# The first attention of a two-block kernel, put in steps between the products of the eight query and key units

## The reference, cut to what matters

```python
def first_block(x, ...):
    h = rms_norm(x, attn_pre_norm)
    x = x + rms_norm(hybrid_mixer(h, ...), attn_post_norm)
    h = rms_norm(x, ffn_pre_norm)
    return x + rms_norm((silu(h @ w_gate) * (h @ w_up)) @ w_down, ffn_post_norm)

def hybrid_mixer(h, ...):
    dq, dk, dv, nq, kc, vc, ks, vs, kw, vw, gt = split(h @ w_in)
    # differential attention: 4 heads, two maps each, values of width 128
    a = softmax(q0 @ k0) - lam * softmax(q1 @ k1)      # causal, queries in blocks of 128
    o_diff = rms_norm(a @ v, diff_subln) * (1 - lam_init)        # head by head
    # sparse attention: 8 query heads in 2 groups, three gated branches
    kcmp, vcmp = compress(kc), compress(vc)            # silu(blocks @ w1) @ w2
    o_nsa = g0 * attn(q, kcmp, vcmp) + g1 * attn(q, ks, vs) + g2 * attn(q, kw, vw)
    return concat([o_diff, o_nsa]) @ w_out
```

## Time and profile before

| | us |
|---|---|
| median of 3 runs (1918.52 to 1919.34) | 1919.23 |
| the profiled execution | 1918.23 |
| its span | 1916.3 |
| PE busy in it | 1875.6 (98%) |
| POOL busy in it | 1241.5 (65%) |
| DVE busy in it | 820.6 (43%) |
| ACT busy in it | 436.3 (23%) |
| mean granted TensorE clock | 0.993 |

### The profile page before, as it was taken

One profiled execution on the slowest core, in us unless ns is written; L12 is line 12 of the kernel. 1 busy time (PEld: TensorE's weight loads), 2 busy tenths in 40 slices (PEclk: granted clock), 3 DMA queues, 4 the chain that ended last, 5 costly groups with the idle time before them and its releaser, 6 DMA issues.

```text
span 1916.3 us, 25712 instructions
## 1 busy us (share of the span) xinstructions
PE 1875.6 (98%) x9416; PEld 1511.1 (79%) x9416; DVE 820.6 (43%) x1396; ACT 436.3 (23%) x893; POOL 1241.5 (65%) x747
## 2 busy tenths in 40 slices
PE   8999999999999999999999999999999999999997
PEld 6886568888888898767888888889787888888886
DVE  6346864533331045253543334004994463334103
ACT  4344862211110021132311111003334331111000
POOL 7975546866676558653876667666656686666662
PEclk9999999999999999999999999999999999999999
DMA  6341002323232214211242323221323223333311
GB/s 207 122 131 45 2 1 78 98 89 99 88 120 96 91 45 154 88 46 44 78 119 89 99 88 126 96 75 56 109 67 99 77 88 97 89 99 108 106 61 44
DMA packets 44878, 168.28 MB, mean 88 GB/s; under 512 B 4984, under 2 KB 7288, under 8 KB 44672
## 3 DMA queue, kind: packets, MB, share of 16 engines
q1 hardware_dynamic: 44496, 164.56, 27.7%
q10 hardware_dynamic: 304, 2.64, 0.4%
HBM read 165.07 MB, written 2.11 MB: 87 GB/s over the span
## 4 chain that ended last, share of the span: by engine, by line
PE 87%; DVE 5%; POOL 5%; issue 2%; ACT 1%; DMA 0%; POOLq 0%; SPq 0%; DVEq 0%
PE psum L527 27%; PE psum L528 26%; PE psum L529 26%; POOL w_lo L421 2%; DVE h_lo L1413 1%; DVE tmp L1455 1%; PE psum L723 1%; DVE e_ring L1570 1%; PE psum L709 1%; POOL w_hi L418 1%; PE psum L574 1%; POOL e_ring L467 1%; PE psum L783 1%; PE psum L804 1%; PE psum L750 1%
## 5 line engine op out<-in xcount | busy, mean ns | idle before, releaser
L421 POOL TENSOR_TENSOR w_lo<-raw,w_hi 128x1024 fp32r<-128x1024 f32 (+1 forms) x286 | 749.6, 2621 | 23.8
L527 PE MATMUL psum<-h_hi,w_hi 128*128 128x512 f32 (+1 forms) x1780 | 677.4, 381 | 13.6 <-POOL w_lo L421 7.1
L529 PE MATMUL psum<-h_hi,w_lo 128*128 128x512 f32 (+1 forms) x1780 | 670.7, 377 | 0.0
L528 PE MATMUL psum<-h_lo,w_hi 128*128 128x512 f32 (+1 forms) x1780 | 670.6, 377 | 0.0
L418 POOL TENSOR_SCALAR w_hi<-raw 128x1024 fp32r<-128x1024 f32 (+1 forms) x286 | 323.0, 1129 | 484.1 <-PE psum L529 460.2
L527 PEld LDWEIGHTS psum<-h_hi,w_hi 128*128 128x128 f32 x1780 | 334.7, 188 | 88.4 <-issue 13.8
L529 PEld LDWEIGHTS psum<-h_hi,w_lo 128*128 128x128 f32 x1780 | 334.1, 188 | 68.9
L528 PEld LDWEIGHTS psum<-h_lo,w_hi 128*128 128x128 f32 x1780 | 334.3, 188 | 66.9 <-issue 0.2
L527 PE MATMUL psum<-g_hi,w_hi 128*128 128x512 f32 (+1 forms) x594 | 219.5, 369 | 0.0
L528 PE MATMUL psum<-g_lo,w_hi 128*128 128x512 f32 (+1 forms) x594 | 218.9, 369 | 0.0
L529 PE MATMUL psum<-g_hi,w_lo 128*128 128x512 f32 (+1 forms) x594 | 218.9, 369 | 0.0
(11 more groups left out here) (269 smaller groups left out, 1858.1 us busy)
## 6 DMA issues: line engine op xcount, KB each, us to landing
raw<-in_wide SPq DMA_DIRECT2D x239, 512.0 KB, 3.6
raw<-in_down SPq DMA_DIRECT2D x48, 704.0 KB, 4.1
decay<-decay_rows ACTq DMA_DIRECT2D x1, 2048.0 KB, 7.9
out<-x SPq DMA_DIRECT2D x16, 128.0 KB, 1.7
x<-in_xt SPq DMA_DIRECT2D x3, 512.0 KB, 7.0
x<-in_xt ACTq DMA_DIRECT2D x1, 512.0 KB, 4.6
o_diff<-in_angles SPq DMA_DIRECT2D x1, 512.0 KB, 10.3
cols<-in_cols SPq DMA_DIRECT2D x1, 221.0 KB, 4.4
```

The lines of the kernel that those rows point to most:

```text
L421: nc.gpsimd.tensor_tensor(w_lo[:, slot, 0:w], raw[:, j % RAW, 0:w], w_hi[:, slot, 0:w].bitcast(F32), ALU.subtract).then_inc(units_split, 1)
L527: pe.matmul(out_ap, lhs[0], rhs[0], start=first, stop=False)
L528: pe.matmul(out_ap, lhs[0], rhs[1], start=False, stop=False)
L529: return pe.matmul(out_ap, lhs[1], rhs[0], start=False, stop=last)
```

## The change

The 32 units come in another order: value units (dv) before the eight query and key units, compression pairs one feature unit apart. The eight units dq0, dk0, dq1, ... dk3 are last, and 42 of the 48 steps are put between their products, at the places `A_WEAVE`; six steps and the rest of the pipeline follow, the last three stages at columns of the opening. Sparse and differential heads alternate. Scores use banks 2 and 3 only, transpositions of differential steps bank 4 only, since banks 0 and 1 serve the units. The four blocks of compressed scores are computed in one go, their softmaxes run one after another, and their transpositions are two calls in dq0. Sparse outputs are written over queries that are no longer needed (`nsa_out`), the angles have a tile of their own. The norm of the differential heads is done head by head: ACT scales three heads with twelve copies, the fourth comes last. `stay_warm` is gone from this stage.

```diff
-A_STREAM = ["kc", "vc", "vg0", "vg1", "vg2", "nq0", "nq1", "nq2", "ck0", "cv0", "nq3", "ks", "ck1", "cv1", "kw", "dq0", "ck2", "cv2",
-            "dq1", "dq2", "ck3", "cv3", "dq3", "dk0", "w2", "dk1", "dk2", "dk3", "dv0", "dv1", "dv2", "dv3"]
+A_WOVEN = [f"{w}{c}" for c in range(4) for w in ("dq", "dk")]
+A_STREAM = ["kc", "vc", "vg0", "vg1", "vg2", "nq0", "nq1", "ck0", "cv0", "nq2", "ck1", "cv1", "nq3", "ck2", "cv2", "ks", "ck3", "cv3",
+            "kw", "dv0", "w2", "dv1", "dv2", "dv3"] + A_WOVEN
...
-STEPS = DIFF_STEPS + NSA_STEPS
+STEPS = nsa_steps(0) + nsa_steps(1) + diff_steps(0) + nsa_steps(2) + diff_steps(1) + nsa_steps(3, (1,)) + diff_steps(2) + nsa_steps(3, (2,)) + diff_steps(3)
+A_WEAVE = [(3, 5, 6, 7)] + [(1, 3, 4, 6, 7)] * 3 + [(1, 2, 3, 5, 6, 7)] * 3 + [(1, 3, 4, 6, 7)]
+A_WOVEN_STEPS = [[sum(map(len, A_WEAVE[:j])) + k for k in range(len(A_WEAVE[j]))] for j in range(len(A_WOVEN))]
+A_LEFT = A_WOVEN_STEPS[-1][-1] + 1
...
@@ POOL: where the weighing stands among the splits
-                    cuts.insert(0, (A_UNITS + SLOTS, weigh_pairs))
+                    first = A_UNITS - len(A_WOVEN) + SLOTS
+                    rest = [A_WOVEN_STEPS[j][-1:] + (A_WOVEN_STEPS[j + 1][:-1] if j + 1 < len(A_WOVEN) else list(range(A_LEFT, len(STEPS))))
+                            for j in range(len(A_WOVEN))]
+                    cuts[0:0] = [(first, lambda: weigh_pairs(A_WOVEN_STEPS[0][:-1]))] \
+                        + [(first + j + 1, lambda steps=steps: weigh_pairs(steps)) for j, steps in enumerate(rest)]
@@ PE: a step
-                        if t >= 2:
-                            pe.wait_ge(pair_maxed, 2 * (t - 1))
-                        elif t == 1:
-                            pe.wait_ge(v_out, len(TOKEN_MAJOR))
-                        stay_warm(warm.get(t, 0), 2 * (t % 2))
+                    if t:
+                        pe.wait_ge(pair_maxed, 2 * t)
+                    else:
+                        pe.wait_ge(v_out, len(TOKEN_MAJOR))
+                    if kind == "diff" and i == NB - 1:
+                        pe.wait_ge(rope_added, ROPES.index(f"dk{head}") + 1)
...
-                        if r >= 2:
-                            copied(r if kind == "nsa" else r - 1)
+                    if r:
+                        copied(r)
@@ PE: the woven units
+            def woven_pairs():
+                low_start = n.base["h_low"]
+                for j, name in enumerate(A_WOVEN):
+                    if name == "dk0":
+                        pe.wait_ge(cmp_turned, 2)
+                    bank, w = free_bank(name), next_unit()
+                    for t in range(KC):
+                        mm = three(psum[:, bank, :], [w[0](t), w[1](t)], h_of(t), t == 0, t == KC - 1)
+                        if t == KC - 1:
+                            mm.then_inc(unit_done, 1)
+                        if t in A_WEAVE[j]:
+                            pair_step(A_WOVEN_STEPS[j][A_WEAVE[j].index(t)], low_start)
+                        if j == 0 and t in (2, 5):
+                            cmp_turn(t // 5)
+                for t in range(A_LEFT, len(STEPS) + 1):
+                    pair_step(t, low_start)
+                pe.wait_ge(rope_added, len(ROPES))
+                pe.wait_ge(pair_maxed, 2 * len(STEPS))
+                def between(t):
+                    if t < 3:
+                        pair_step(len(STEPS) + 1 + t, low_start)
+                    if t == 2:
+                        turn_diff(0)
+                        turn_diff(1)
+                        turn_diff(2)
+                    if t == 5:
+                        turn_diff(3)
+                w_out((4, 5, 6, 7, 0, 1, 2, 3), nsa_of, between)
@@ PE: the order ahead of them
-            feature("nq2")
             compress(0)
+            feature("nq2")
+            compress(1)
             feature("nq3")
+            compress(2)
             feature("ks")
-            compress(1)
+            compress(3)
             feature("kw")
-            feature("dq0")
...
             for u in token_units("dv", (2, 2, 2, 2), 4 * P):
-                if u in (1, 2):
-                    cmp_turn(u)
-                    cmp_scores(u + 1)
-            cmp_turn(3)
+                if u == 0:
+                    second_layer()
+                if u == 1:
+                    cmp_scores()
+            woven_pairs()
@@ ACT: after dv3
+            for j, name in enumerate(A_WOVEN):
+                for k, t in enumerate(A_WOVEN_STEPS[j]):
+                    if j == 0 and k == 0:
+                        cmp_copy(0)
+                    if j == 0 and k == 1:
+                        cmp_copy(1)
+                    if t == A_WOVEN_STEPS[j][-1]:
+                        shift(name)
+                    pair_step(t)
+            for t in range(A_LEFT, len(STEPS) + PAIR_MIX + 2):
+                pair_step(t)
+                if t == len(STEPS):
+                    diff_root(0, slice(0, 12))
+                if t == len(STEPS) + 1:
+                    scale_diff()
+            turned_high(0)
+            diff_root(1, slice(12, 16))
+            for c in range(1, 4):
+                turned_high(c)
@@ DVE: after the four cmp_softmax
+            for j, name in enumerate(A_WOVEN):
+                for t in A_WOVEN_STEPS[j][:-1]:
+                    pair_step(t)
+                rope_parts(name)
+                pair_step(A_WOVEN_STEPS[j][-1])
+                rope_sum(name)
+            for t in range(A_LEFT, len(STEPS) + PAIR_MIX + 1):
+                pair_step(t)
...
```

More of the change, by code:

```diff
@@ L144, in combined_by_dve, with done_before @@
     return STEPS[t][0] == "diff" and STEPS[t][3] == NB - 1
+def done_before(kind, head):
+    place = next(j for j, end in enumerate(SET_ENDS) if end[1:] == (kind, head))
+    earlier = [end for end in SET_ENDS[:place] if MIX_BANK[end[1:]] == MIX_BANK[kind, head]]
+    return earlier[-1][1:] if earlier else None
 def copies_by_dve(upto):
@@ L605, in last_unit, with opening @@
                 mm.then_inc(unit_done, 1)
-            def opening(order, h):
+            def opening(order, h, before=None):
                 banks, units = [], []
@@ new lines, in diff_root, with scale_diff @@
+            def diff_root(k, sums):
+                act.wait_ge(diff_mean, k + 1)
+                nc.scalar.activation(diff_ms[:, 2, sums], diff_ms[:, 3, sums], ACT.Sqrt).then_inc(diff_rooted, 1)
+            def scale_diff():
+                act.wait_ge(diff_inverted, 1)
+                for head in range(3):
+                    for b in range(NB):
+                        part = dqk[:, head, b * P:(b + 1) * P]
+                        ins = copy(part, part, scale=diff_ms[:, 1, 4 * head + b:4 * head + b + 1])
+                    ins.then_inc(diff_normed, 1)
@@ L1637, in fox_step @@
                     n.take("h_low")
-            def turn_outputs(first, banks, scale=None):
-                for c in range(4):
-                    low_of_bank(first + c, 4 + c % banks, scale)
             v.memset(ones[:], 1.0).then_inc(set_up, 1)
```

480 lines of the change are left out of this document (239 added, 241 removed).

## The result

The changed kernel takes 1925.29 us (median of 7 runs, 1924.12 to 1925.99), the kernel before 1918.96 (7 runs on the same chip, 1917.95 to 1920.49): 1.0032 times as long, with an interval of 1.0020 to 1.0043. That is 6.3 us slower, at a forecast of 11.6 us slower. The profiled execution took 1925.33 us, span 1923.5.

The account below looks back on a forecast made before the run. TensorE, with 87% of the chain, was taken as the bound, with 14 us to win in the first attention. -14 - 0.6 + 9.7 + 5.9 + 4.2 + 6.4 = +11.6 us, about 1930; range 1920 to 1937.

Parts of the forecast that it names:

- Idle time of the stage: First attention stage: TensorE's ramp, warming calls and most waits for softmax work go, minus 14 us.
- The short products: Value and key units before the weaving: four small insertions shrink to one, minus 0.6 us.
- Part 1: Woven units and opening: 46 insertions between products cost about 0.21 us each, 9.7 us; between 0 and 14.
- the trace has the same weaving in the second attention: Step giving the price per insertion: gaps of 0.09 and 0.11 us there, about 0.2 us, taken for every insertion.
- The sign that I named: What would show the insertion price: each woven step shows 0.32 and 0.34 us around it, where the pace is 0.233.
- Rival (b): Stepping in is free: sum +1.9 us, 1921, no change; 0.09 together with a faster case, 0.02 of it faster.
- Part 2: Units before the weaving: waits for low tokens and GpSimd splits plus a half clock delay kw, 5.9 us; 4.8 to 7.
- Part 3: Woven stretch: waits at the start 0.9, at unit ends 1.5, for differential weighing 1.8; sum 4.2 us.
- Part 4: Tail, steps 42 to 49 without products: TensorE waits for maxima, copies and weighings, 6.4 us; between 3 and 10.
- (a): All waits of TensorE covered: minus 4.9 us, 1914, faster; chance 0.08.
- (c): Tail and unit boundaries cost a third of the forecast: +4.6 us, 1924, on the border of no change; chance 0.18.
- (d): Woven stretch: DVE's sparse-step coefficient is locked out by GpSimd's split, +8 us if half shows, 1938; chance 0.15.

Follow-up runs that it names:

- e3: Kernel after plus 24 unread transpositions in the attention's output projection, one behind each triple of three feature units: 1927.66 us.
- e4: Kernel after plus the same 24 unread transpositions in one row behind the three feature units: 1927.59 us.
- e8: Kernel after plus unread small operations of three kinds between triples of the output projection's feature units, then eight of each kind in a row; one profile, not timed.
- e10: Kernel after with the mix ahead of the transposition in each attention step: 1925.85 us, ratio 1.0039 to the kernel before.
- e1: Kernel after with nq2 ahead of the first compress pair, kw ahead of the fourth, hidden-layer turn inside the first value unit: 1924.28 us, ratio 1.0035 to the kernel before.
- e5: Kernel after with ScalarE copying the transposed block before the rotation's shift in each of eight woven units: 1925.92 us, ratio 1.0040 to the kernel before.
- e7: On top of the order of e1, ScalarE makes the high part of the eight compress units instead of POOL: 1920.48 us, ratio 1.0009 to the kernel before.
- e6: Kernel after with VectorE combining the last differential head's two softmaxes, one instruction a step for all four blocks: 1922.89 us, ratio 1.0025 to the kernel before.
- e9: Kernel after with the 64 short products in four stretches of 16, each behind one value-unit tile: 1925.11 us, ratio 1.0034 to the kernel before.
- e2: Kernel after with the 64 short products split, 32 behind the second and 32 behind the third value unit: 1923.72 us, ratio 1.0035 to the kernel before.
- e12: e11 with mix first only in the 42 woven steps, ScalarE's copy ahead of the shift, and two filling products: 1915.68 us, ratio 0.9984 to the kernel before.
- e11: Kernel after with the edits of e1, e7, e9, e6 and e10 together: 1921.51 us, ratio 1.0016 to the kernel before.

## Why the prediction came out as it did

**Direction right, size high by 5 us.** The parts, forecast against measured:

- Idle time of the stage: -14 forecast. In the kernel before it is 10.2 us of stands and 3.4 of warming, so -13.6; the prediction's "14" was rounded up.
- The short products: -0.6 forecast, -1.5 measured. Four stretches of 16 with three turns of the compressed branch between them, and the second layer of the compression, cost TensorE 8.7 us among the products before; the row of 64, one turn and the second layer cost 7.2 after, with 0.9 for the lower clock inside the row in it.
- Part 1, stepping in: +9.7 forecast, about +6 measured. The mechanism was half right. 28 steps end in a sparse mix and pay 0.17 to 0.19 each, some 5; three at the start, with a score alone, pay some 0.2. Steps with a differential mix, cmp_turn and the three stops in the opening pay nothing. The failed step is "the trace has the same weaving in the second attention": there every step ends in a mix on half of the columns, and I carried its price to steps that do not. e3, e4 and e8 showed it, e10 confirmed it by moving the mix. The sign that I named, 0.32 and 0.34 around a step, is there around differential steps too (0.33 and 0.32 around the one at 242.55), which cost nothing: the gaps beside a step are not its price; only its length with and without the products is. Rival (b), stepping in is free, is wrong for 31 of 46 insertions and right for the rest.
- Part 2, units before the weaving: +5.9 forecast, +5.95 measured (87.5 for kw, against 81.55). The two waits and the half clock are as told. But e1 shows that they do not add up as separate costs: GpSimd's pace bounds the stretch, and without the wait for the tokens 2.2 us come back at the first value unit and 1.1 at the short products.
- Not foreseen: the clock behind the short products, +2.3. I had counted the four small insertions made into one as a gain of 0.6 and did not ask what a row of 64 products of 31 columns does to the clock. In three of nine profiles this costs half as much, so part of it is chance.
- Part 3, waits in the woven stretch: +4.2 forecast, +1.9 measured. The copy behind the shift is there; the wait at the start and for the differential weighing never showed. Both appear as soon as TensorE comes earlier: 1.15 us at the first score in e1, 0.58 for the weighing in e5. They were covered by what went wrong ahead of them.
- Part 4, the tail: +6.4 forecast, +5.9 measured: 4.4 us of stands and 1.5 by which the half clock stretched TensorE's work (15.32 us busy from score 42 on, 13.80 in e3). In e3, with the clock up, the stands alone are 5.9 us. From the end of the last unit to the opening it took 284.44 - 262.68 = 21.8 us, which is the forecast 15.4 and 6.4. The stands are largely those named (score 42 0.45 for 0.9; transposition 39 1.13 for 1.1; the differential weighing 1.88 for 1.55). The stand of 1.9 for a weighing behind the split is not in this profile; e7 and e8 have it, with 1.40. Here the split did its harm another way, through VectorE's coefficient.

-13.6 - 1.5 + 6 + 5.95 + 2.3 + 1.9 + 5.9 = 6.95, and the two profiles are 7.0 us apart behind the output projection. The 0.6 us that the kernel after wins back behind that are not explained. The opening starts at 283.6 (less the 0.85) and not near 291: 2.6 of the 7.0 us lie behind its first product, where the turns of the heads now stand. That the size was high is the price of stepping in and the woven waits (6.0 us too much together); the unforeseen clock hid 2.3 us of this, so the total is nearer to its forecast than the parts deserve.

**The rivals.** (a) is out: the waits were there. (c), a third of the tail and boundaries, did not happen either (6.3 us of stands of 10.6), though the time came close to its 1924, for other reasons. (d) has its mechanism but not its price: four coefficients in the profile after take over 1 us (178.43, 181.13, 268.38 and 271.27), and VectorE has time for the first two; only the tail pays, 0.8 us. The Trainium skill, SBUF — State Buffer, section Who interferes with whom, has it that whoever starts first on the shared ports holds them for its whole instruction; the pair at 268.37 and 268.38 agrees. The pair of e8, both at 268.62, starts too close together to say who was first.

**Open.** The same stand of 1.67 us before kw is followed by 3.4 us at the lower clock in two profiles (e6, e9) and by none in seven others (after, e2, e3, e4, e5, e8, e10); the stand of 1.89 before nq0, which every profile has, by 3.4 us in two (e7, e12); and the tail has none, one or two such falls. What decides it I can't say. A fall among products costs up to 1.7 us, and such falls go with the scatter of e11. What made the rest of the gain of e7 in time is open too.

## What to carry to other kernels

When small matmuls are woven between large ones, look at the part of the array each uses: in this kernel every change between full, half-row and half-column operands costs 0.17 to 0.2 us, and a transposition or a full product between large products costs only itself, so end an insertion with an operation of the full array. Before moving short units closer together, add up the pace of the engine that prepares their operands; the waits that it causes are one budget, and removing one of them shows the next. Before you call an edit useless, follow its gain along the chain to the place where it ends: e5 and e10 gained nothing in time by themselves, one for a fall of the clock in the last microseconds and the other for new stands and a longer fall, and together with e6, e7, the order and the quarters they made a kernel 2.8 us faster than the one before.

## What the runs showed of the hardware that was not expected

- 64 products of 31 columns in a row, with TensorE busy all the time, go with 6.8 us at a granted clock of 0.50 (1.2 GHz) in six profiles and 3.4 us in three; 32 in a row with 3.4 us or none; 16 with none in the twelve stretches of e9, e11 and e12. The Trainium skill, TensorE: Matmul & The Clock Gate, section What's actually happening, tells the fall as one for lack of activity; here it came with TensorE busy throughout.
- Two fp32 products on 64 rows cost 0.25 us in a row and 0.62 between split products; a full fp32 product 0.235 and 0.22.
- A half clock inside a chain bound by another engine cost nothing: the score of step 44 came 228.15 us after nq0 with it and 228.03 (e6) without. Behind the last stand of the tail it cost e5 0.9 of its 0.95 us.
- A coefficient of 0.16 us on VectorE and a split on GpSimd that start within 10 ns of each other: the coefficient took 2.36 us in the kernel after and 0.16 in e8, with the same code.
